# Gate and up blocks of the feed-forward stages as 512-column products in two banks, with the weight splits placed between reading and taps

## The reference

```python
def conv_glu_ffn(h, w_up, conv_w, conv_b, w_down):
    u = causal_dwconv(h @ w_up, conv_w) + conv_b
    gate, up = jnp.split(u, 2, axis=-1)
    return (jax.nn.silu(gate) * up) @ w_down
```

## Time and profile before

| | |
|---|---|
| median of 3 runs | 1096.36 us (1095.55 to 1097.67) |
| the profiled execution | 1096.5 us, span from the first to the last instruction 1094.7 us |
| PE busy | 1060.8 us (97% of the span) |
| DVE busy | 806.2 us (74%) |
| ACT busy | 595.7 us (54%) |
| granted TensorE clock | 0.995 of full speed on average |

### The profile page before, as it was taken

One profiled execution on the slowest core, in us unless ns is written; L12 is line 12 of the kernel. 1 busy time (PEld: TensorE's weight loads), 2 busy tenths in 40 slices (PEclk: granted clock), 3 DMA queues, 4 the chain that ended last, 5 costly groups with the idle time before them and its releaser, 6 DMA issues.

```text
span 1094.7 us, 22114 instructions
## 1 busy us (share of the span) xinstructions
PE 1060.8 (97%) x9086; PEld 1037.6 (95%) x9086; DVE 806.2 (74%) x1135; ACT 595.7 (54%) x783; POOL 5.3 (0%) x15
## 2 busy tenths in 40 slices
PE   6999999999999999998999999999999899999996
PEld 6999998999999999998999999989999899999995
DVE  5965678777886786767978777779775797777775
ACT  6652546564555464436655445677665555554563
POOL 0000000000000000000000000000000000000000
PEclk9999999999999999999999999999999899999999
DMA  8421232454545554554655555444444254555431
GB/s 329 156 77 40 78 117 83 164 193 135 211 166 188 194 181 160 189 195 150 202 167 184 192 191 187 154 154 154 155 125 148 95 191 175 196 187 192 157 113 39
DMA packets 25714, 174.23 MB, mean 159 GB/s; under 512 B 3069, under 2 KB 3349, under 8 KB 5296
## 3 DMA queue, kind: packets, MB, share of 16 engines
q1 hardware_dynamic: 25088, 171.57, 45.2%
q0 software_dynamic: 560, 1.70, 0.5%
HBM read 172.20 MB, written 1.06 MB: 158 GB/s over the span
## 4 chain that ended last, share of the span: by engine, by line
PE 71%; DVE 7%; ACT 3%; issue 2%; DVEq 0%; ACTq 0%
PE PS L446 39%; PE PS L483 32%; DVE w_lo L1838 2%; ACT w_hi L1210 2%; DVE arena L2424 1%; ACT arena L1590 1%; DVE arena L2428 1%; DVE arena L2442 1%; DVE x L2360 0%; PE PS L1122 0%; DVE arena L2354 0%; DVE h_lo L1851 0%; ACT xn L1266 0%; DVE arena L2356 0%; DVE arena L2456 0%
## 5 line engine op out<-in xcount | busy, mean ns | idle before, releaser
L1838 DVE TENSOR_TENSOR w_lo<-raw,w_hi 128x2048 fp32r<-128x2048 f32 x158 | 361.3, 2288 | 71.2 <-ACT w_hi L1210 69.5
L446 PE MATMUL PS<-h_hi,w_hi 128*128 128x256 f32 x1248 | 355.4, 285 | 2.6 <-DVE w_lo L1838 2.5
L446 PE MATMUL PS<-h_lo,w_hi 128*128 128x256 f32 x1248 | 353.1, 283 | 0.0
L446 PE MATMUL PS<-h_hi,w_lo 128*128 128x256 f32 x1248 | 353.1, 283 | 0.0
L1210 ACT ACTIVATE w_hi<-raw 128x2048 fp32r<-128x2048 f32 x158 | 300.6, 1905 | 85.4 <-PE PS L483 45.2
L446 PEld LDWEIGHTS PS<-h_hi,w_hi 128*128 128x128 f32 x1248 | 239.4, 192 | 4.4 <-issue 3.9
L446 PEld LDWEIGHTS PS<-h_lo,w_hi 128*128 128x128 f32 x1248 | 239.4, 192 | 0.3 <-issue 0.2
L446 PEld LDWEIGHTS PS<-h_hi,w_lo 128*128 128x128 f32 x1248 | 239.4, 192 | 0.0
L483 PE MATMUL PS<-act_hi,w_hi 128*128 128x256 f32 x720 | 202.1, 282 | 1.2 <-DVE act_lo L1868 1.2
L483 PE MATMUL PS<-act_hi,w_lo 128*128 128x256 f32 x720 | 202.3, 282 | 0.0
L483 PE MATMUL PS<-act_lo,w_hi 128*128 128x256 f32 x720 | 199.7, 283 | 0.0
(11 more groups left out here) (311 smaller groups left out, 1304.4 us busy)
## 6 DMA issues: line engine op xcount, KB each, us to landing
raw<-weights SPq DMA_DIRECT2D x158, 1024.0 KB, 4.9
arena<-masks_in SPq DMA_DIRECT2D x1, 1856.0 KB, 14.1
raw<-weights SPq DMA_DIRECT2D x2, 512.0 KB, 5.9
x<-x_in SPq DMA_DIRECT2D x4, 256.0 KB, 7.1
arena<-bias_by_distance POOLq DMA_DIRECT2D x1, 1024.0 KB, 7.7
result<-x SPq DMA_DIRECT2D x4, 256.0 KB, 2.1
arena<-p_in POOLq DMA_DIRECT2D x2, 256.0 KB, 4.3
row<-row_in SPq DMA_DIRECT2D x1, 326.0 KB, 10.2
```

The lines of the kernel that those rows point to most:

```text
L446: return pe.matmul(o, lhs, rhs, start=start, stop=stop)
L1838: tt(w_lo[:, slot, :], raw[:, slot, :], w_hi[:, slot, :].bitcast(F), ALU.subtract).then_inc(lo_ready, 1)
```

## The change

In each feed-forward stage the blocks gate 2 and gate and up of pairs 3 to 10 are made by `wide_columns`: 17 blocks a stage. `h_hi` and `h_lo` become two halves of one tile, `h_both`, so that one matmul of 512 columns multiplies a `w_hi` piece with both. The tile f of a block now has a bank of its own: columns 0 to 255 take high x high and, from a second matmul of 256 columns, `w_lo` x `h_hi`; columns 256 to 511 take high x low. A gate block lies in banks 4 and 5, an up block in 6 and 7, for every pair. Up 2 stays a `columns` block and goes to bank 6 instead of 5.

Reading a wide block takes three steps: ACT copies the second halves of both banks to a new tile `low` (`low_part`), DVE adds the first halves and `low`, and DVE multiplies by `r_x`. `gate_read` and `up_read` are signalled by the multiply. There is one tile `low`; ACT waits for DVE's add before it writes it again.

In `triple` the splits are those of G+3, G+4 and G+5. The first comes after the gate is read and before its taps, the second after up is read and before its taps, the third after the product and before the hidden split. The block n0+9 (`ahead(n0 + 7)`) is split at the end of the entry, and `ahead(n0 + 31)` at the end of the stage is dropped, since the loop has done it. Five semaphores that were used once are merged into two.

```diff
-        h_hi = sb("h_hi", [P, KC, TOK], R)
-        h_lo = sb("h_lo", [P, KC, TOK], R)
+        h_both = sb("h_both", [P, KC, 2, TOK], R)
+        h_hi, h_lo = h_both[:, :, 0, :], h_both[:, :, 1, :]
...
+        low = place([P, 2, TOK])
...
+            def wide_columns(n0, slot, bank):
+                block_ready(n0)
+                for f in range(2):
+                    o = PS[:, bank + f, :]
+                    for k in range(KC):
+                        at = k * 256 + f * P
+                        add(o, w_hi[:, slot, at:at + P], h_both[:, k, :, :].rearrange("p b n -> p (b n)"), k == 0)
+                        last = add(o[:, 0:TOK], w_lo[:, slot, at:at + P], h_hi[:, k, :], False, k == KC - 1)
+                last.then_inc(block_used, 1)
...
-                def triple(n, at, pairs_done, odd, first=False):
-                    bank = 6 if odd else 4
-                    pe.wait_ge(sem("gate_read"), pairs_done)
-                    columns(n, slot(at), bank, (h_hi, h_lo))
-                    pe.wait_ge(sem("up_read"), pairs_done)
-                    columns(n + 1, slot(at + 1), bank + 1, (h_hi, h_lo))
+                def triple(n, at, pairs_done, odd):
+                    pe.wait_ge(sem("gate_read"), pairs_done + 1)
+                    wide_columns(n, slot(at), 4)
+                    pe.wait_ge(sem("up_read"), pairs_done + 1)
+                    wide_columns(n + 1, slot(at + 1), 6)
                     pe.wait_ge(sem("hidden_split"), pairs_done)
-                    channel_rows(n + 2, slot(at + 2), hid[odd], 0, first, False)
-                triple(n0 + 4, 4, PAIRS * f + 1, 0, True)
+                    channel_rows(n + 2, slot(at + 2), hid[odd], 0, False, False)
+                pe.wait_ge(sem("gate_read"), PAIRS * f + 1)
+                pe.wait_ge(sem("up_read"), PAIRS * f + 1)
+                wide_columns(n0 + 4, slot(4), 4)
+                pe.wait_ge(sem("gate_read"), PAIRS * f + 2)
+                columns(n0 + 5, slot(5), 6, (h_hi, h_lo))
+                pe.wait_ge(sem("hidden_split"), PAIRS * f + 1)
+                channel_rows(n0 + 6, slot(6), hid[0], 0, True, False)
...
+                def low_part(bank, n_used, copied):
+                    act.wait_ge(block_used, n_used)
+                    if not isinstance(copied, int) or copied > 1:
+                        act.wait_ge(sem("parts_added"), copied - 1)
+                    act.activation(low, PS[:, bank:bank + 2, TOK:512], ACT.Copy).then_inc(sem("low_copied"), 1)
...
                 def triple(q, n_base, step, i, odd):          # ACT
-                    split_of(n_base + 2, step, i)
+                    low_part(4, n_base + 1 + step * i, 2 * q + (WIDE * f - 4))
+                    split_of(n_base + 3, step, i)
                     gate(q)
-                    split_of(n_base + 3, step, i)
+                    low_part(6, n_base + 2 + step * i, 2 * q + (WIDE * f - 3))
+                    split_of(n_base + 4, step, i)
                     up(q)
-                    split_of(n_base + 4, step, i)
-                    act.wait_ge(block_used, n_base + 3 + step * i)
+                    split_of(n_base + 5, step, i)
                     hid_part(q, odd)
...
                 ahead(n0 + 6)
+                low_part(4, n0 + 5, WIDE * f + 1)
                 hid_part(1, 1)
...
                 up(2)
-                act.wait_ge(block_used, n0 + 7)
+                ahead(n0 + 7)
                 hid_part(2, 0)
...
-                ahead(n0 + 31)
                 ahead(n0 + 32)
...
+                def read_wide(z, bank, done, q, n_used, copied):
+                    dve.wait_ge(block_used, n_used)
+                    dve.wait_ge(sem("low_copied"), copied)
+                    tt(z, PS[:, bank:bank + 2, 0:TOK], low, ALU.add).then_inc(sem("parts_added"), 1)
+                    dve.wait_ge(sem("parts_added"), copied)
+                    tt(z, z, units(r_x[:, 0:TOK], 2), ALU.mult).then_inc(done, 1)
+                    dve.wait_ge(done, q + (PAIRS * f + 1))
...
                 def triple(q, n_base, step, i, odd):          # DVE
-                    bank = 6 if odd else 4
-                    split_of(n_base + 2, step, i)
-                    read(z_gate, bank, sem("gate_read"), q, n_base + 1 + step * i)
+                    read_wide(z_gate, 4, sem("gate_read"), q, n_base + 1 + step * i, 2 * q + (WIDE * f - 4))
+                    split_of(n_base + 3, step, i)
                     gate(q)
-                    split_of(n_base + 3, step, i)
-                    read(z_up, bank + 1, sem("up_read"), q, n_base + 2 + step * i)
+                    read_wide(z_up, 6, sem("up_read"), q, n_base + 2 + step * i, 2 * q + (WIDE * f - 3))
+                    split_of(n_base + 4, step, i)
                     up(q)
-                    split_of(n_base + 4, step, i)
+                    split_of(n_base + 5, step, i)
                     hid_part(q, odd)
...
-                read(z_gate, 4, sem("gate_read"), 2, n0 + 5)
+                read_wide(z_gate, 4, sem("gate_read"), 2, n0 + 5, WIDE * f + 1)
                 hid_part(1, 1)
...
                 ahead(n0 + 6)
-                read(z_up, 5, sem("up_read"), 2, n0 + 6)
+                read(z_up, 6, sem("up_read"), 2, n0 + 6)
                 up(2)
+                ahead(n0 + 7)
                 hid_part(2, 0)
...
-                ahead(n0 + 31)
```

More of the change, by code:

```diff
@@ L86 @@
 T_PARTS = 5
+WIDE = 1 + 2 * (PAIRS - 3)
 ONCE = {
@@ L95 @@
     "grams": ("decay_logs", "qk_gram", "decay_turned", "m_turned"),
+    "bias_by_act": ("bias_rows", "bias_copied", "lambda_exps"),
+    "bias_by_pe": ("bias_by_head", "bias_flipped"),
     "constants": ("eps_set", "ones_set", "zeros"),
@@ L431, in _ @@
             pool.dma_start(p_tok, p_in[0]).then_inc(sem("p_loaded"), 16)
-            pool.wait_ge(sem("bias_rows"), 1)
+            pool.wait_ge(*once("bias_rows"))
             pool.dma_start(bias_dram, bias_row).then_inc(sem("bias_stored"), 16)
@@ L1057, in _ @@
                     pe.wait_ge(sem("sc_gc"), 4)
-                    mm(PS[0:N_HEADS, 5, 0:N_DIST], table, onehot).then_inc(sem("bias_by_head"), 1)
+                    mm(PS[0:N_HEADS, 5, 0:N_DIST], table, onehot).then_inc(once("bias_by_head")[0], 1)
                 pe.wait_ge(sem("sc_hidden"), j + 1)
@@ L1097, in _ @@
                 last = mm(PS[:, b, :], flip, bias_rev[:, 2 * b:2 * b + 2, :].rearrange("p h n -> p (h n)"))
-            last.then_inc(sem("bias_flipped"), 1)
+            last.then_inc(once("bias_flipped")[0], 1)
             def logits(h):
@@ L1113, in turn_weights @@
                 if h == 0:
-                    pe.wait_ge(sem("bias_copied"), 1)
+                    pe.wait_ge(*once("bias_copied"))
                 if h == 6:
@@ L1663, in _ @@
                 ahead(STEP["sc_out"] + j)
-            act.wait_ge(sem("bias_by_head"), 1)
-            act.activation(bias_row, PS[0:N_HEADS, 5, 0:N_DIST], ACT.Copy).then_inc(sem("bias_rows"), 1)
+            act.wait_ge(*once("bias_by_head"))
+            act.activation(bias_row, PS[0:N_HEADS, 5, 0:N_DIST], ACT.Copy).then_inc(once("bias_rows")[0], 1)
             squares_of_y(2, 0, STEP["sc_out"] + 4)
@@ L1756, in _ @@
             ahead(a0 + 2)
-            act.wait_ge(sem("bias_flipped"), 1)
-            act.activation(flat(bias_t), PS[:, 0:4, :].rearrange("p b n -> p (b n)"), ACT.Copy).then_inc(sem("bias_copied"), 1)
+            act.wait_ge(*once("bias_flipped"))
+            act.activation(flat(bias_t), PS[:, 0:4, :].rearrange("p b n -> p (b n)"), ACT.Copy).then_inc(once("bias_copied")[0], 1)
             act.wait_ge(sem("lambda_sums"), 1)
-            act.activation(lam[:, 0:2], lam[:, 0:2], ACT.Exp).then_inc(sem("lambda_exps"), 1)
+            act.activation(lam[:, 0:2], lam[:, 0:2], ACT.Exp).then_inc(once("lambda_exps")[0], 1)
             ahead(a0 + 3)
@@ L2597, in lambda_minus @@
             def lambda_minus():
-                dve.wait_ge(sem("lambda_exps"), 1)
+                dve.wait_ge(*once("lambda_exps"))
                 link(tt(lam[:, 2:3], lam[:, 1:2], lam[:, 0:1], ALU.subtract))
@@ L2622, in head @@
                 if h == 0:
-                    dve.wait_ge(sem("bias_copied"), 1)
+                    dve.wait_ge(*once("bias_copied"))
                 for m in range(2):
```

## The result

The changed kernel takes 1082.49 us (median of four runs, 1080.42 to 1084.17) against 1096.4 us for the kernel before on the same chip (1095.55 to 1097.67): the ratio is 0.9872, with a 95% interval of 0.9855 to 0.9889. The profiled execution took 1081.21 us, its span is 1079.4, which is 15.3 less than before.

What follows compares the result with a forecast made beforehand. The prediction took TensorE (PE), busy 97% of the span, as the bound. Wide matmuls 1.6 us plus entry stalls 3.9 us made 5.5 less than 1096.5, giving 1091.0 us, range 1088 to 1094.

Steps and rivals of the forecast that it cites:

- I take 238, close to the upper stored row: Wide blocks: a 512-column matmul takes 238 ns, near the 0.24 us of one of two `level_masks` matmuls streaming stored values.
- I read this as a limit on how fast stored fp32 values stream in, which a wide instruction doesn't lift: Matmuls with stored operands: 120 ns for 256 columns is a streaming rate, 0.469 ns a column, so 240 for 512.
- rival (a): Wide blocks: a fixed price for each matmul with its load, 512 columns in 227 to 230 ns; 1084.3 us, chance 0.17.
- 816 x 2 ns = 1.6 us: Wide blocks: 816 steps go from 360 to 358 ns each, saving 1.6 us; bounds 19.6 us and nothing.
- the broadcast rows: Three earlier 512-column matmuls, gd_hi and gd_lo, streaming an operand with step 0, starting 0.21 to 0.22 us before the next.
- The entry stalls: Stage entries: PE waits for `w_lo` at gate n0+10 and up n0+11; 3.9 us saved over three stages, bounds zero and 3.9.
- The timetable: First stage's entry: forecast times of reads, taps and splits against PE's needs; up of pair 2 read 1.5 us early.
- rival (c): Neither pays: 512 columns take 240 ns and later taps (1.8 us) keep the entry stalls; 1096.4 to 1094.5 us, chance 0.11.
- The new reads: Wide-block reads: copy, add, multiply stay hidden under PE; DVE 13.1 to 14.5 us a triple; bare they would cost 66.
- Rival (d): Feed-forward triples: DVE becomes the bound, over 17.3 us a triple, with copy and taps' waits bare; 1097 to 1109, chance 0.09.
- Rival (b): Wide blocks: the full width pays, 216 + 120 = 336 ns a step, saving 19.6 + 3.9 us; 1072.9 us, chance 0.12.

Runs made afterwards that it cites:

- the first experiment: The changed kernel with each wide step made again of three 256-column matmuls, same banks, reads and order of splits: 1094.27 us, ratio 0.9978 to the kernel before.

## Why the prediction was wrong

**The step that failed** is "I take 238, close to the upper stored row", and behind it "I read this as a limit on how fast stored fp32 values stream in, which a wide instruction doesn't lift". A stored stream does cost more than one with step 0, but mostly by an amount for each matmul and not for each column: beyond columns/2.4 it is 16 ns for 512 columns and 12 for 256 in runs of one width, where a rate asks for 27 and 13. In turns the two take 346.9 ns together, 230.1 and 116.7, where 358 were forecast and rival (a) put 350. So the term "816 x 2 ns = 1.6 us" measured 10.3 us by the stages. Of the 13.0 ns a step, 9.9 are the wide matmul at 230 instead of 240, which is what rival (a) said; the other 3.3 are its 256-column partner at 116.7 instead of 120, which neither the forecast nor a rival had, and which is why the time lies below (a) as well. The mechanism was in the main rival (a), which had 0.17.

The argument against (a) was that "the broadcast rows ... carry a load and no such price". It excluded a price of the load; it didn't exclude one of the instruction that only some operands have. The number for the forecast came from two start times outside a long stream, and the prediction had named it as its weakest. It was not an error of rounding: to the nanosecond the two rows are 230 and 239 ns, and the changed kernel has the same spread, 230 in the loops and a mean of 236 in block gate 2. The forecast took one end of that spread for the value of the long stream.

**The entry stalls** were right in place and in size: 3.9 us taken, 4.0 measured (1.56, 1.21 and 1.19 against 1.54, 1.19 and 1.18). The timetable held within 0.6 to 0.9 us, everything earlier than forecast, 0.5 of it because the stage itself began at 224.07 instead of 224.54. The first add came at 249.60 (forecast 250.2), the taps at 252.18 (252.9), `w_lo` of n0+8 was done at 256.2 (256.8), up of pair 2 was read by 256.8 (257.6), `w_lo` of n0+9 done at 262.7 (263.6), n0+10 at 267.1 (268), n0+11 at 272.6 (273.3). No margin was used up, so rival (c) has neither of its halves.

**The new reads** were right: 14.5 us of DVE a triple, hidden, with room for 0.7 more at each read. **Rival (d)** did not occur in the changed kernel. With the splits in their old places the time, 1103.9 us, lies in its range of 1097 to 1109, but its mechanism, triples of over 17.3 us, holds for one stage of three; in all three the larger part was lost at the entry.

**Rival (b)** asked for 336 ns. The Trainium skill ("TensorE: Matmul & The Clock Gate", Back-to-back issue gap) gives an estimate of 216 ns for 512 columns; the runs agree for a stream with step 0, at 216.6, and disagree for stored values, at 230.

**The sum.** The stages give 4.0 + 10.3 = 14.3 us of the span's 15.3. The other 1.0 lies between the stages: the first starts 0.5 earlier, and the 92 matmuls before the third took 14.36 us before and 13.19 after, those before the second 11.68 and 12.23. The windows in the first experiment show the granted clock behind all four, 0.79 and 0.87, 1.00 and 0.95. The start of the first stage lies between 223.5 and 224.8 us over the twelve traces, so its 0.5 us is no effect of the change either. The change itself is worth the 14.3.

What stays open: why a stored stream costs a matmul 10 to 17 ns beyond its columns and one with step 0 less, why the 256-column matmul is quicker behind a wide one, why the first wide block of a stage is slower than the others, and why loads of 64 columns are quicker than those of 128 and of 32.

## What to carry to other kernels

Before a change of width, split the time of a matmul into columns/2.4 and a remainder: from one width alone a price for each instruction and a slower rate look the same, so the two ends must both keep a fair chance until a stream of another width has been timed, over many instructions and not from two start times. What a neighbour costs can change with it: here the unchanged 256-column matmul gave a quarter of the saving. A saving on the engine that is full pays only if the engine that feeds it keeps the new pace: here the wider products alone made the kernel slower, and the order of the feeding engine's list, worth 4 us alone, turned that into a gain of 14 us. Most of what the old order lost lay at the entries, where that engine was late, and not in the steady loop. A right total does not confirm a theory: read where the time went. To find out whether added work is hidden, add half as much again and read the stage.

## What the runs showed of the hardware

- fp32r matmuls with stored operands take more than columns/2.4 by an amount that doubling the width does not double: in runs 119.0 ns for 256 columns and 229.7 for 512 (12 and 16 ns more), in turns 116.7 and 230.1 (10 and 17). With the streamed operand at step 0 the pair takes 329.8 ns instead of 346.9.
- A matmul of four columns with its own 128-column load adds 112.5 ns to a full stream, the same as its distance to the next in the earlier trace rows.
- Weight loads of 64 columns make the pair 340.5 ns, those of 32 columns 347.2, those of 128 columns 346.9.
- The granted clock over the same 92 matmuls was between 1.00 and 0.79 in different traces and stages, and their time between 11.68 and 14.36 us; it varies between executions of one kernel.
